# 32-bit products of probabilities and values on two column halves of TensorE, and their sums on GpSimd

## What is computed

```python
logits = q @ k.T * scale + cum[lo:hi, None] - cum[None, :hi]     # per head, query block lo:hi
logits = where(s_pos <= t_pos, logits, -inf)
p = softmax(logits)
o = p @ v[:hi]
y = o * silu(z)
```

## Time and profile before

| | us |
|---|---|
| median of three runs | 1587.24 (1586.86 to 1590.64) |
| the profiled execution | 1583.64 |
| its span | 1581.8 |
| TensorE busy | 1528.9 (97%) |
| VectorE busy | 934.3 (59%) |
| ScalarE busy | 690.4 (44%) |
| GpSimd busy | 629.3 (40%) |

### The profile page before, as it was taken

One profiled execution on the slowest core, in us unless ns is written; L12 is line 12 of the kernel. 1 busy time (PEld: TensorE's weight loads), 2 busy tenths in 40 slices (PEclk: granted clock), 3 DMA queues, 4 the chain that ended last, 5 costly groups with the idle time before them and its releaser, 6 DMA issues. The chain is left out here.

```text
span 1581.8 us, 22045 instructions
## 1 busy us (share of the span) xinstructions
PE 1528.9 (97%) x7762; PEld 1223.1 (77%) x7762; DVE 934.3 (59%) x1564; ACT 690.4 (44%) x1307; POOL 629.3 (40%) x540
## 2 busy tenths in 40 slices
PE   7999999999999999999989999998999999989998
PEld 5888888888888888888866776776777777667886
DVE  7455555555415766920237786676678677646755
ACT  0346364544511111131115776766676777831100
POOL 2212121121221111111116888877797888921111
PEclk9999999999999999999988999999999999999999
DMA  6134335251584333326525646453546455324642
GB/s 258 47 117 138 109 100 147 73 173 60 154 133 127 120 105 122 100 73 142 164 94 151 183 125 185 140 145 102 153 127 168 140 154 174 88 77 136 193 131 93
DMA packets 190657, 206.48 MB, mean 131 GB/s; under 512 B 50940, under 2 KB 134140, under 8 KB 187516
## 3 DMA queue, kind: packets, MB, share of 16 engines
q1 hardware_dynamic: 189972, 203.24, 44.7%
q10 hardware_dynamic: 576, 1.84, 0.4%
HBM read 129.79 MB, written 75.17 MB: 130 GB/s over the span
## 5 line engine op out<-in xcount | busy, mean ns | idle before, releaser
L1507 POOL TENSOR_TENSOR m_p_lo<-m_p,m_p_hi 128x512 fp32r<-128x512 f32 (+1 forms) x320 | 374.5, 1192 | 60.6 <-ACT m_p_hi L1471 58.3
L554 PE MATMUL bank<-x_hi,w_hi 128*128 128x512 f32 x992 | 394.2, 397 | 0.0
L554 PE MATMUL bank<-x_hi,w_lo 128*128 128x512 f32 x992 | 387.1, 390 | 0.0
L554 PE MATMUL bank<-x_lo,w_hi 128*128 128x512 f32 x992 | 386.2, 389 | 0.0
L579 POOL TENSOR_TENSOR w_lo<-w_raw,w_hi 128x512 fp32r<-128x512 f32 x64 | 93.8, 1486 | 479.0 <-ACT w_hi L638 479.0
L1469 ACT ACTIVATE m_p<-m_st,fcol 128x512 f32<-128x512 f32 (+1 forms) x320 | 203.9, 637 | 139.1 <-PE m_st L1349 64.1
L554 PEld LDWEIGHTS bank<-x_hi,w_lo 128*128 128x128 f32 x992 | 186.2, 188 | 40.2
L554 PEld LDWEIGHTS bank<-x_lo,w_hi 128*128 128x128 f32 x992 | 186.6, 188 | 36.4
L554 PEld LDWEIGHTS bank<-x_hi,w_hi 128*128 128x128 f32 x992 | 186.5, 188 | 35.8
L1471 ACT ACTIVATE m_p_hi<-m_st,fcol 128x512 fp32r<-128x512 f32 (+1 forms) x320 | 202.2, 632 | 0.0
L1563 DVE TENSOR_REDUCE m_maxima<-m_aux 128x1 f32<-128x512 f32 x192 | 130.1, 685 | 63.5 <-PE m_aux L1326 58.3
(11 more groups left out here) (214 smaller groups left out, 2584.6 us busy)
## 6 DMA issues: line engine op xcount, KB each, us to landing
w_raw<-in_w SPq DMA_DIRECT2D x31, 512.0 KB, 3.8
dram_feat<-ring SPq DMA_DIRECT2D x48, 256.0 KB, 4.0
arena<-dram_gates SPq DMA_DIRECT2D x32, 256.0 KB, 4.8
o_y<-dram_mixT SPq DMA_DIRECT2D x16, 512.0 KB, 6.2
o_x<-in_x SPq DMA_DIRECT2D x16, 512.0 KB, 4.2
out<-o_res SPq DMA_DIRECT2D x15, 512.0 KB, 5.0
arena<-in_xT SPq DMA_DIRECT2D x7, 1024.0 KB, 9.5
K<-dram_k_hi SPq DMA_DIRECT2D x12, 512.0 KB, 7.3
```

Source lines behind the costliest of these rows:

```text
L554: mm = pe.matmul(banks[bank_of(s)][:], w[:, i % 2, k * P:(k + 1) * P], x[:, k, b * BLOCK:(b + 1) * BLOCK], start=(k == 0 and n == 0), stop ...
L1507: pool.tensor_tensor(p_lo[(s - 1) % PL][:, off:], p[(s - 1) % PL][:, off:], p_hi[(s - 1) % PH][:, off:].bitcast(F32), ALU.subtract).then_i ...
```

## The change

- **Products.** `values(last)` runs once in four slots and does four units in a row (`QUAD`). Each unit is one full 32-bit product of 64 value columns with all of `p`, where it was three fp32r ones. Even key blocks add into partitions 0 to 63 of the bank, odd ones into 64 to 127. `LAG` goes from 3 to 2, and `p` becomes a ring of eight. `p_hi`, `p_lo`, `v_hi`, `v_lo` and the column of ones are gone, and with them the second exponential, GpSimd's subtraction and VectorE's subtraction for `v_lo`.
- **Sums.** GpSimd adds each unit's `p` to a 128 x 512 total of its group. The first two units of a group are added in one instruction; for that, the second unit of a first query block is computed in all its 512 columns. After the group an auxiliary item `den` follows: TensorE turns the total (four transposes), VectorE sums along the rows into 128 x 4 and inverts.
- **The group's end.** ScalarE copies the odd half out of the bank, VectorE adds the even half, GpSimd multiplies by the gate. The reciprocals are stored in pieces of one element; the DMA that spread the sums is gone.

```diff
-LAG = 3
-ST, PH, PL = 2, 4, 3
+LAG = 2
+QUAD = 4
+ST, PL = 2, 8
-SPREAD, INVERT, GATHER, SPREAD_BACK, RESCALE = 1, 6, 7, 11, 15
+SUMS, GATHER, SPREAD_BACK, RESCALE = 1, 4, 9, 14
...
+        put(last_unit(G) + LAG + SUMS, ("den", G))
...
 def unit(s):
     h, g, kb = UNITS[s]
     d = kb - 4 * g
-    off = P * min(max(d, 0), 2)
-    return h, g, kb, off, d >= 0, slice(0 if d == 3 else P, 2 * P)
+    first = g == 0 and d == 1
+    off = 0 if first else P * min(max(d, 0), 2)
+    return h, g, kb, off, d >= 0, slice(0 if d == 3 or first else P, 2 * P)
+def adds_through(s):
+    u = s if UNITS[s][2] else s + 1
+    return u + 1 - sum(first_unit(G) <= u for G in range(N_GROUPS))
...
             def _(sp):
-                        if G < N_GROUPS - 1 and s == done_at + SPREAD:
-                            sp.wait_ge(den_ready, G + 1)
-                            sp.dma_start(dens[G % 2][:], den[G % 2][:].rearrange("o (p j) -> o p j", j=512 // FD))\
-                              .then_inc(dens_landed[G % 2], 16)
                         if G < N_GROUPS - 1 and s == done_at + GATHER:
                             sp.wait_ge(recs_ready, G + 1)
-                            sp.dma_start(rec_rows[G].rearrange("(p j) -> p j", j=512 // FD), recs[G % 2][:]).then_inc(recs_stored, 16)
+                            sp.dma_start(rec_rows[G].rearrange("(a p) -> p a", p=P), recs[G % 2][:], allow_slow_non_contiguous=True)\
+                              .then_inc(recs_stored[G % 2], 16)
...
             def _(pe):
+                    elif kind == "den":
+                        G = what[0]
+                        pe.wait_ge(p_added, adds_through(last_unit(G)))
+                        for a in range(4):
+                            mm = pe.transpose(b[:, a * P:(a + 1) * P], acc[G % 2][:, a * P:(a + 1) * P], ident[:])
...
-                def values(s):
-                    pe.wait_ge(p_hi_ready, s + 1)
-                    pe.matmul(b[0:FD + 1, off:], v_hi[i % 2][:, kb, j, :], p_hi[s % PH][:, off:], start=kb == 0, stop=False)
-                    pe.matmul(b[0:FD, off:], v_lo[i % 2][:, kb, j, :], p_hi[s % PH][:, off:], start=False, stop=False)
-                    pe.wait_ge(p_lo_ready, s + 1)
-                    pe.matmul(b[0:FD + 1, off:], v_hi[i % 2][:, kb, j, :], p_lo[s % PL][:, off:], start=False,
-                              stop=kb == 4 * g + 3).then_inc(pv_done, 1)
+                def values(last):
+                    for s in range(last - QUAD + 1, last + 1):
+                        h, g, kb, off, diagonal, _ = unit(s)
+                        G = h * NB + g
+                        i, j = divmod(h, 2)
+                        half = slice(kb % 2 * FD, (kb % 2 + 1) * FD)
+                        if kb == 0:
+                            done(pe, both_ready, G - 2)
+                            pe.wait_ge(v_ready, 4 * i + g + 1)
+                        pe.wait_ge(p_ready, s + 1)
+                        pe.matmul(pv[G % 2][half, off:], v[i % 2][:, kb, j, :], p[s % PL][:, off:], start=kb < 2,
+                                  stop=kb >= 4 * g + 2).then_inc(pv_done, 1)
...
-                    if 0 <= s - LAG < N_UNITS:
+                    if 0 <= s - LAG < N_UNITS and (s - LAG) % QUAD == QUAD - 1:
                         values(s - LAG)
...
             def _(act):
+                    if 0 <= s - 1 - LAG < N_UNITS and s - 1 - LAG == last_unit(group_of(s - 1 - LAG)):
+                        G = group_of(s - 1 - LAG)
+                        act.wait_ge(pv_done, last_unit(G) + 1)
+                        done(act, both_ready, G - 2)
+                        act.activation(odd[G % 2][:], pv[G % 2][FD:P, :], ACT.Copy).then_inc(odd_ready, 1)
...
-                    done(act, p_lo_ready, s - PL)
+                    if s >= PL:
+                        act.wait_ge(pv_done, s - PL + 1)
+                        act.wait_ge(p_added, adds_through(s - PL))
                     act.activation(p[s % PL][:, off:], st[s % ST][:, off:], ACT.Exp, bias=bias).then_inc(p_ready, 1)
-                    done(act, pv_done, s - PH)
-                    act.activation(p_hi[s % PH][:, off:], st[s % ST][:, off:], ACT.Exp, bias=bias).then_inc(p_hi_ready, 1)
...
             def _(pool):
-                        pool.tensor_tensor(p_lo[(s - 1) % PL][:, off:], p[(s - 1) % PL][:, off:],
-                                           p_hi[(s - 1) % PH][:, off:].bitcast(F32), ALU.subtract).then_inc(p_lo_ready, 1)
+                        pool.wait_ge(p_ready, u + 1)
+                        total = acc[G % 2][:, off:]
+                        if kb == 1:
+                            if G >= 2:
+                                pool.wait_ge(aux_ready, AUX_INDEX["den", G - 2] + 1)
+                            pool.tensor_tensor(total, p[(u - 1) % PL][:], p[u % PL][:], ALU.add).then_inc(p_added, 1)
+                        else:
+                            pool.wait_ge(p_added, adds_through(u) - 1)
+                            pool.tensor_tensor(total, total, p[u % PL][:, off:], ALU.add).then_inc(p_added, 1)
+                    if 0 <= s - 2 - LAG < N_UNITS and s - 2 - LAG == last_unit(group_of(s - 2 - LAG)):
+                        pool.wait_ge(both_ready, G + 1)
+                        pool.wait_ge(zb_landed[G % 2], 16 * (G // 2 + 1))
+                        done(pool, yb_ready, G - 4)
+                        pool.tensor_tensor(gated[G % 4][:], both[G % 2][:], zb[G % 2][:], ALU.mult).then_inc(gated_ready, 1)
...
             def _(dve):
-                        dve.tensor_copy(v_hi[i % 2][:, cut, :, 0:FD], src).then_inc(v_hi_ready, 1)
-                        dve.wait_ge(v_hi_ready, 4 * i + blk + 1)
-                        dve.tensor_tensor(v_lo[i % 2][:, cut, :, :], src, v_hi[i % 2][:, cut, :, 0:FD].bitcast(F32), ALU.subtract)\
-                           .then_inc(v_ready, 1)
+                        dve.tensor_copy(v[i % 2][:, cut, :, 0:FD], src).then_inc(v_ready, 1)
...
+                    elif kind == "den":
+                        dve.reduce_sum(dens[G % 2][:], b[:].rearrange("p (a k) -> p a k", k=P), AX.X).then_inc(aux_used, 1)
+                        dve.wait_ge(aux_used, m + 1)
+                        dve.reciprocal(recs[G % 2][:], dens[G % 2][:]).then_inc(recs_ready, 1)
...
+                def finish(G):
+                    dve.wait_ge(odd_ready, G + 1)
+                    done(dve, gated_ready, G - 2)
+                    dve.tensor_tensor(both[G % 2][:], pv[G % 2][0:FD, :], odd[G % 2][:], ALU.add).then_inc(both_ready, 1)
```

More of the change, by code:

```diff
@@ L1104, in mix @@
         v_feat = home["v_feat"]
-        v_hi.append(sb("v_hi1", [P, NCH, 2, FD + 1], F32R))
-        v_lo.append(sb("v_lo1", [P, NCH, 2, FD], F32R))
+        v.append(sb("v1", [P, NCH, 2, FD]))
         p = [sb(f"p{i}", [P, 512]) for i in range(PL)]
-        p_hi = [sb(f"p_hi{i}", [P, 512], F32R) for i in range(PH)]
-        p_lo = [sb(f"p_lo{i}", [P, 512], F32R) for i in range(PL)]
         maxima = sb("maxima", [P, 4, 4])
@@ L1113, in mix @@
         neg_max = sb("neg_max", [P, 4], F32R)
-        den = [sb("den0", [1, 512]), scr["den"]]
-        dens, recs = ([sb(f"{n}0", [FD, 512 // FD]), scr[n]] for n in ("dens", "recs"))
+        acc = [sb(f"acc{i}", [P, 512]) for i in range(2)]
+        odd = [sb(f"odd{i}", [FD, 512]) for i in range(2)]
+        both = [sb(f"both{i}", [FD, 512]) for i in range(2)]
+        dens, recs = ([sb(f"{n}0", [P, 4]), scr[n]] for n in ("dens", "recs"))
         rec_b = [sb("rec_b0", [FD, 512]), scr["rec_b"]]
@@ L1475, in _ @@
                 pool.memset(ones_r[:].bitcast(F32), 1.0)
-                for i in range(2):
-                    pool.memset(v_hi[i][:, :, :, FD:].bitcast(F32), 1.0)
                 pool.memset(half[:], -0.5)
@@ L1502, in _ @@
                 for s in range(END_SLOT + 1):
[L1503 to L1508 removed]
+                    if 0 <= s - 1 < N_UNITS and UNITS[s - 1][2] > 0:
+                        u = s - 1
+                        _, _, kb, off, _, _ = unit(u)
+                        G = group_of(u)
+                        pool.wait_ge(p_ready, u + 1)
[8 more added lines that the diff above has]
+                    if 0 <= s - 2 - LAG < N_UNITS and s - 2 - LAG == last_unit(group_of(s - 2 - LAG)):
+                        G = group_of(s - 2 - LAG)
+                        if G == 0:
+                            for i in range(RING):
+                                pool.wait_ge(scr["ring_stored"][i], 16 * len(range(i, RING_AT[N_SLOTS], RING)))
+                        pool.wait_ge(both_ready, G + 1)
+                        pool.wait_ge(zb_landed[G % 2], 16 * (G // 2 + 1))
+                        done(pool, yb_ready, G - 4)
+                        pool.tensor_tensor(gated[G % 4][:], both[G % 2][:], zb[G % 2][:], ALU.mult).then_inc(gated_ready, 1)
                     for item in AUX_AT.get(s - 1, ()) if s > 0 else ():
@@ L1648, in _ @@
                 for s in range(END_SLOT + 1):
```

(7 more changed lines are left out.)

76 lines of the change are left out of this document (25 added, 51 removed).

## The result

The changed kernel takes 1616.11 us (median of 4 runs, 1608.49 to 1620.01) against 1587.05 us for the kernel before on the same chip (1586.2 to 1590.64): a ratio of 1.0173, interval 1.0132 to 1.0214. The whole interval lies above 1, so it is slower; the forecast was 1573, with a range up to 1604. The profiled execution took 1617.47 us, its span 1615.7.

A forecast was written before the change was run, and what follows sets the result against it. TensorE's stream of matmuls was taken as the bound, with GpSimd 81% busy behind it. Terms of -48.0 + 6 + 11.5 + 1 + 15 gave -14.5 us, a median of 1573 us, range 1540 to 1604.

The forecast's parts named there:

- Items 1 and 2: Mixing-stage products: removing three per unit saves 194.4 us; adding one 32-bit product costs 155.6, five steps per four units.
- Rival B: Mixing-stage products: column halves fully overlap, a pair costing two steps, 31.7 us less; 1545 us, chance 0.20.
- Item 3: TensorE's turns between full array and a half: 0 to 14 us over 80 groups, 6 taken.
- Item 4: Sums of probabilities: transposes add 11.5 us, wider scores 1 us; waiting for the last addition costs nothing.
- Item 5: Other engines beside TensorE: GpSimd 463 us busy and hidden; SP's store of reciprocals in 4-byte pieces costs nothing.
- Item 6: New TensorE waits from uneven slots, at the chunk's steps: 0 to 39 us, 15 taken.
- Item 7: End of the mixing stage, before projection out: nothing net, 1 us either way.
- The last sentence of the prediction: Forecast wrong if its signs hold but the time doesn't, for instance if the granted clock, 0.97, falls with the unevenness.

The follow-up runs named there:

- run 1: Changed kernel with the reciprocals stored in 128 pieces of 16 bytes instead of 512 of 4, order permuted; 1583.57 us, 0.9971 of the kernel before.
- run 3: Changed kernel with neighbouring key blocks sharing a column half, except in groups of a first query block; 1627.72 us, 1.0248 of the kernel before.
- run 7: On top of run 1, each 32-bit product takes both heads' 128 value columns, filling the whole array; 1651.1 us, 1.0388 of the kernel before.
- run 5: On top of run 1, ScalarE instead of GpSimd makes the diagonal of maxima; 1586.49 us, 0.9988 of the kernel before.
- run 10: Changed kernel with 16-byte reciprocal stores in the right order, each transpose taking every fourth query; 1586.45 us, 0.9973 of the kernel before.
- run 6: On top of run 1, products are made for two units at a time instead of four; 1588.53 us, 1.0009 of the kernel before.
- run 8: Changed kernel with sums by a ones product on TensorE, no reciprocals' trip over DRAM, gates loaded later; 1703.31 us, 1.0728 of the kernel before.

## Why the prediction was wrong

Sums below are taken from one matmul's start to the next, between the first and the last scores: 565 us before, 564 in run 1, 595 after.

- **Items 1 and 2, the products.** Rival B, given 0.20, was right about them: full overlap, four steps. The failed argument is "starts follow program order": A's second pass starts after B's first, at a diagonal even after B's second (the records of a group come 512, 384, 384, 512 wide), and in run 3 the halves pair up over another order still. The step of 0.43 us was right (run 7). So 31.7 us were there to be had beyond the forecast. The Trainium skill, TensorE: Matmul & The Clock Gate, Part 3, says that small tiles run concurrently: the starts 6 ns apart agree. Its rule that matmuls start and end in strict program order does not hold here between two column tiles.
- **Item 3, the turns.** Forecast 6 us, measured 80 x 0.34 = 27. The rows of 65, 64 and 65 columns were the wrong neighbour: they show no such cost, the 32-bit halves do; whether the 64-column product there changed the tiling at all, no run shows. The dearest row there gave 14 at most, so the bound was too low as well. The Trainium skill, TensorEngine Tiling (Array Packing), Key Properties, says that changing the tiling mode drains TensorE; priced in the prediction at 26 us and set aside. For the halves the measured 27 us agree with that; in the 65-64-65 products no such cost shows.
- **Item 4.** The transposes take 11.5 to 11.7 us, as forecast (11.5). "No cost" for the wait on the last addition holds inside the stage (0.6 us), but not for the last group, where nothing else is left: 5.9 us (L1341 in the waits above). The two slots behind the last unit are no cover when they are the last.
- **Item 5, the store.** This is the step that put the result outside the range. "It lands while SP goes on for five slots (7 us) against 1.7 to 5.6 us for the store now"; "at worst the loads queued behind it (queries of two groups later) slip, with slots to spare. Nothing." The price was taken from a store in larger pieces; in 4-byte pieces it is 10.3 us, past the five slots. The slots to spare were spent as well: ahead of the load at 1099.49 us SP stood still for 7.6 and 2.4 us at L1259, 3.7 at L1271 and 2.3 at L1218, one after the other. And the forecast had no term for what a store in flight does to the loads beside it (7.6 us to land in place of 3.1). Cost by runs 1 and after: 32 us, of which 18.6 are idle time and 12 are work at half the clock (71.6 us of work at the lower level against 47.6, half of the difference). GpSimd's busy time was right (458 against 463) and the engine is no bound.
- **Item 6, the new waits.** With the store mended TensorE is idle 37.1 us. Without the 9.2 that went, 15.5 of before's 24.7 would be left, so 21.6 are new; the forecast took 15, and E1, O and QS, where it put them, hardly wait. They are at the diagonal of maxima (17.1 us against 5.7 before, both between 815 and 1440 us) and at the loads of QM (12.1 against 4.0), parts of the schedule that the change did not touch. When ScalarE makes the diagonal (run 5) the wait falls to 4.1 us, and others take its place. What the forecast had no term for is the clock: 47.6 us of work at the lower level against 29.3, so 9 us.
- **Item 7.** From the last score product to the first product of the projection out is 10.5 us in run 1, 7.35 before: 3 us, forecast "nothing net".

The sum with measured terms: -14.5, then -31.7 + 21 for items 2 and 3, +6.6 for the waits, +9 for the clock, +3 for the end, makes -6.6 us; run 1 has -4.6 (0.9971). With the store's 32 that is +25; measured +29. The match is in part luck. The terms come from two profiled executions, and between these the span grows by 4.3 us (1581.8 to 1586.1): the one of run 1 took 4.3 us more than its median, the one before 3.4 less. Their work at the full clock between the first and the last scores is 526.2 and 503.3 us, 22.9 less, where items 1 to 4 with measured terms give 31; 8 us of work have no term. So the change is a good product bought with turns, waits and clock at nearly its whole price, and one store that makes it a loss. The last sentence of the prediction named the clock as what could break it; it should have been a term: in run 1, five of the six dips that begin between the first and the last scores begin within 5 us of the start of an idle stretch of 2.1 to 6.7 us.

Still open: how much of the 0.34 us lies in draining before, and how much in refilling behind; and whether a schedule with the diagonal of maxima given out earlier would win back what is waited there. Neither was tried.

## What to carry to other kernels

When an edit changes a DMA's access pattern, price it by the size of its pieces and not by its bytes alone, find what is queued behind the first wait for it, and look at what the transfers beside it then take. Price work in parts of the array with a cost for each entry, and put many units behind one entry. A wait on the bounding engine can cost more than its length: in run 1, 12.4 us more of idle time came with 9 us for longer dips of the clock.

## What the runs showed of the hardware

- 2 KB written as 512 pieces of 4 bytes land in 10.3 us (7.5 to 14.8), as 128 of 16 bytes in 3.9 (2.0 to 10.3; run 10: 3.6), with the same other transfers in the program. The kernel before's 64 pieces of 32 bytes land in 2.4. The loads of QM land in 7.6, 4.5 and 3.1 us in these three kernels.
- Two 32-bit products in different column halves run at the same time, both passes: a step of 512 columns is 0.43 us alone and paired (the first of a group 0.47), and out of program order between the halves.
- Entering and leaving the halves costs 0.34 us a group (after, run 6), while 32-bit products in the whole array cost nothing beyond their passes (run 7).
- VectorE's reciprocal takes 1751 ns for 64 x 256 elements (run 8), 6.8 ns per element of a partition; its sum over 512 elements takes 0.67 us (after, L1606).
